# First mixture of experts: the down product fed in row slices one step behind the up product, summed by VectorE, with TensorE's program written out

## The chip, the cores and the metric

One Trainium2 chip, one of its cores. The metric is the time of one execution on the device in microseconds (us); lower is better. Everything is float32. TensorE ("PE" in the rows; "PEld" is its loading of weights) multiplies, VectorE ("DVE") and ScalarE ("ACT") work elementwise, GpSimd is "POOL", and SyncE ("SP") here does little but issue transfers from the chip's memory (HBM).

## The reference, cut to what matters

The program is a two-layer block (attention, feed-forward, attention, mixture of 8 experts), followed by a second block with a mixture of 32 small experts. The change touches only the first mixture, with 256 tokens of width 1024, hidden width 2816, two experts per token:

```python
logits = (x2 @ w_router).astype(jnp.float32) + b_router.astype(jnp.float32)
top_vals, top_idx = lax.top_k(logits, TOP_K)
gates = jax.nn.softmax(top_vals, axis=-1)
...
def expert_block(args):
    xb, e = args
    h = xb @ w_in[e]
    return (jax.nn.silu(h[:, :D_FF]) * h[:, D_FF:]) @ w_out[e]
...
y = jnp.zeros_like(x2).at[slot_tok].add((ys * slot_gate[:, None]).astype(x2.dtype))
```

All weights of an expert are read whatever its number of tokens: 1024 x 5632 and 2816 x 1024 floats, 22 and 11 times 1024 KB.

## The kernel before

Expert `e` has room for `CAPS[e]` tokens (80, 84, 60, 76, 64, 72, 68, 72). For each expert TensorE runs, in this order:

- **gather** (L1114, in `gather`): a 0/1 matrix picks the tokens' columns into `XG`, two more transposes turn the gates (L1119).
- **up** (L1166, in `up_half`, called by `up_pairs`): 11 steps `f`. Each uses 2 MB of weights `ein`, as two transfers of 1 MB (`x` = 0, 1), and makes 256 hidden columns and their 256 partners. The 1 MB slots of `IN1` are four, two steps deep. ScalarE applies silu (L2725), VectorE multiplies by the partner (L1715, `hn`), and all 22 hidden tiles are kept in `HT`.
- **down** (L1188, in `down`, called by `down_fours`): 8 steps `d`. Each uses 1408 KB of `eout`, which holds 128 output columns of all 2816 rows, and sums over all 22 hidden tiles inside PSUM, so it can't begin before the last up step. Its result is copied out by ScalarE (even `d`, `even_dims`) or VectorE (odd `d`, L2094). The slots `OUT1` are four.
- **turn** (L1148) and **scatter** (L821): the result is transposed back to tokens and multiplied by the gates; VectorE adds it to `Y`. They belong to expert `e - 1` and run inside expert `e`.

Each matrix product is issued as two halves of 64 output rows, and the profile has two MATMUL records for one product (the halves of float32). An expert has 1408 MATMUL records of up and 704 of down, and the same number of weight loads.

TensorE's program holds two loops per expert. `up_pairs` writes out two steps `f` and repeats them five times; `down_fours` writes out four steps `d` and repeats them twice. Waits inside the loops compare semaphores with registers that count up:

```python
with pe.Fori(16 * (5 * e + 1), 16 * (5 * e + 6), 16) as landed:
    for f in (1, 2):
        pe.wait_ge(hnD.sem, hid)
        for x in range(2):
            pe.wait_ge(loop_in[in_slot(f, x)], landed)
            up_half(e, f, x).then_inc(inP.sem, 1)
```

SyncE issues the transfers in one fixed order, each after a wait for its slot: for every expert all 22 transfers of `ein`, then all 8 of `eout` (`load_in`, L3084; `load_out`, L3088). The slots lie in `ringbuf`, which in the stages ahead of the mixture is a ring of four 2 MB slots; `cleared` names the product after which each of those is free. For the first expert four `ein` and two `eout` transfers are issued ahead, and `in_free(0, 0, x)` waits for ring slot 0, which the last product ahead of the mixture (the attention's output product, `wo`) empties last.

Of the kernel before, what the change touches and what calls it, by code (L numbers as in the profile page):

```python
# [16 lines left out]
NE1 = 8  # L17
# [266 lines left out]
def build(nc, dr, out, dbg=None):  # L284
    ctx = ExitStack()
    with ctx:
# [43 lines left out]
        F = lambda a: a.rearrange("p a b -> p (a b)")  # L330

# [22 lines left out]
        PGT = [ar(2048 + 256 * (e % 2), 256)[0:n, :] for e, n in enumerate(CAPS)]  # L354
        XG = [ar(2560 + 1024 * (e % 2), 8, n) for e, n in enumerate(CAPS)]
        HT = [ar(4608, 22, n) for n in CAPS]
        YT = [ar(7424, 8, max(CAPS))[:, :, 0:n] for n in CAPS]
        YS = [ar(8448 + 1024 * (e % 2), 1024)[0:n, :] for e, n in enumerate(CAPS)]
# [98 lines left out]
        ytA, ytD = [sig(n, ["free"] + [(e, i) for e in E8 for i in range(4)]) for n in ("yt_even", "yt_odd")]  # L457
        htA = sig("ht", [(2, q) for q in Q8])
        dnP = sig("exp_out", [(1, e, d) for e in E8 for d in range(8)] + [(2, q, i) for q in Q8 for i in range(2)])
# [102 lines left out]
        ring = Chunks(plan, slots1, s_ring, where, ends[2], (NE1, NE1, 2 * NE1, 2 * NE1))  # L562
        assert nu == ends[2] and ends[2] % RING != 3


        IN1 = [ringbuf[:, 2048 * k:2048 * k + 2048] for k in range(4)]
        OUT1 = [ringbuf[:, 8192 + DFF * k:8192 + DFF * k + DFF] for k in range(4)]
        first_in, loop_in = s_ring[0:2], s_ring2[0:4]
        loop_out = [s_ring[2], s_ring[3], s_ring2[4], s_ring2[5]]
        cleared = [plan[max(i for i in range(nu) if where[i] == k)][3] for k in range(RING)]  # L570
        at_loop = [max(v for s_, v in ring.value[0:nu] if s_ is s_ring[k]) for k in range(RING)]
        at_first, at_out = at_loop[0:2], at_loop[2]
        assert at_loop[2] == at_loop[3]

        def in_slot(f, x):
            return 2 * (f % 2) + x

        def in_free(e, f, x):

            if e == 0 and f < 2:  # L580
                return cleared[f % 2]
            return inP.at((1, e, f - 2, x) if f >= 2 else (1, e - 1, 10 if f == 0 else 9, x))

        def out_free(e, d):

            if e == 0 and d < 4:
                return cleared[3 if d else 2]
            return dnP.at((1, e, d - 4) if d >= 4 else (1, e - 1, 4 + d))

        loop_free = [inP.at((1, NE1 - 1, 10, 1)), inP.at((1, NE1 - 1, 9, 1)), dnP.at((1, NE1 - 1, 5)), dnP.at((1, NE1 - 1, 6))]  # L590
# [7 lines left out]
        base = [16 * 5 * NE1] * 4 + [max(n_ for s_, n_ in ring.value if s_ is s_ring[k]) for k in last] + [16 * 2 * NE1] * 2  # L598
# [31 lines left out]
        def plan_o1(e):  # L630
            return ([(dr["ein"][e, i].rearrange("x p n -> p x n"), SLOT) for i in range(11)],
                    [(dr["eout"][e, d], DFF) for d in range(8)])
# [173 lines left out]
        def tensor_program(pe):  # L806
# [325 lines left out]

            slot_ranks(1, NE1, cnt1)
            busy(1, 6)
            busy(1, 6, 256)
            gather(1, 0, [seD.at((1, 0))] * 2, PS, PG, XG)

            def turn(e):

                for h in range(2):  # L1140
                    pe.wait_ge(*ytA.at((e, 2 * h + 1)))
                    pe.wait_ge(*ytD.at((e, 2 * h + 1)))
                    if e + 1 < NE1:
                        pe.wait_ge(*(xgD.at((1, e + 1, 1)) if h else pgA.at((1, e + 1))))
                    else:
                        pe.wait_ge(*ctD.at(h))
                    for k in range(4):
                        ins = pe.transpose(PB[6 + h][0:CAPS[e], k * 128:(k + 1) * 128], YT[e][:, 4 * h + k, :], ident)  # L1148
                    ins.then_inc(*tuP.up((1, e, h)))

# [2157 lines left out]
```

## Time and profile before

| | |
|---|---|
| median of 3 runs | 1914.29 us (1910.86 to 1917.29) |
| the profiled execution | 1919.28 us, span 1917.4 us |
| busy share of the span | TensorE 91%, its weight loads 71%, VectorE 27%, ScalarE 13%, GpSimd 8% |
| first mixture | from 535.9 us to 1242.9 us of the span, 707 us |
| read there | 176 transfers of 1024 KB and 64 of 1408 KB, 276.8 MB |
| TensorE's granted clock | 0.99 in the mixture (full is 2.4 GHz) |

Times of rows are from the start of the span. "issue" as what ended an idle time means that the engine waited for nothing that the profile shows. The profile lists DMA queue by queue: q1 carries what SyncE issues, and the queue of the kind "instruction" carries the engines' own programs.

### The profile page before, as it was taken

To read this page: it belongs to the slowest core of one execution; us is meant where nothing else is said; L and a number is where in the kernel's file an instruction comes from. 1 tells how busy PE (TensorE), PEld (TensorE's weight loads), DVE (VectorE), ACT (ScalarE), POOL (GpSimd) and SP (SyncE) were. 2 spreads that over 40 slices of the span, in tenths; PEclk is the share of its full clock that TensorE was granted. 3 is DMA by queue.
4 is the path that set the end of the run, shared out by engine and by line. 5 is a ranking of instruction groups with operands and counts; after the bars stand their busy time and mean duration, and the time that the engine had idled before them with its cause. 6 is when DMAs were issued, how large, how long until landed. Compare 5 with 4: busy or idle time off the path is not lost.

```text
span 1917.4 us, 53202 instructions
## 1 busy us (share of the span) xinstructions
PE 1736.9 (91%) x24496; PEld 1359.0 (71%) x24496; DVE 520.8 (27%) x1257; ACT 249.8 (13%) x657; POOL 159.9 (8%) x307
## 2 busy tenths in 40 slices
PE   8999999999889998899889898899989989989775
PEld 7758885467489997788788888687657778643331
DVE  1641000233321111110101010246764343232223
ACT  2321000032101000000000000022133112010001
POOL 0000000000007400000000000065430000000000
PEclk9999999999999999999999999989989999999988
DMA  7225444241198999999999999932211028579996
GB/s 315 99 88 198 157 151 151 94 168 71 54 404 361 368 386 405 382 411 382 411 382 406 416 401 407 395 123 67 77 47 44 35 78 372 201 320 429 429 429 280
DMA packets 62950, 498.23 MB, mean 260 GB/s; under 512 B 7097, under 2 KB 15825, under 8 KB 17105
## 3 DMA queue, kind: packets, MB, share of 16 engines
q1 hardware_dynamic: 52672, 490.12, 63.6%
q10 hardware_dynamic: 10128, 5.97, 1.1%
q8 instruction: 111, 1.82, 0.4%
q14 instruction: 39, 0.31, 0.0%
HBM read 495.00 MB, written 1.05 MB: 259 GB/s over the span
## 4 chain that ended last, share of the span: by engine, by line
PE 70%; DMA 21%; DVE 4%; issue 3%; ACT 1%; ACTq 1%; SPq 0%; DVEq 0%
DMA ringbuf<-in_ein 13%; PE pb L812 11%; PE pb L1166 9%; PE pb L1188 8%; PE pb L821 7%; PE pb L817 5%; PE pb L885 3%; PE pb L1070 3%; DMA cst<-in_e2in 2%; PE pb L1387 2%; PE pb L1364 2%; PE pb L1653 2%; DMA ringbuf<-in_e2in 2%; PE pb L1114 2%; DMA ringbuf<-in_eout 2%
## 5 line engine op out<-in xcount | busy, mean ns | idle before, releaser
L1166 PE MATMUL pb<-arena,ringbuf 128*64 128x72 f32 (+6 forms) x11264 | 392.9, 229 | 50.7 <-DMA ringbuf<-in_ein 36.5
L1166 PEld LDWEIGHTS pb<-arena,ringbuf 128*64 128x64 f32 x11264 | 374.6, 138 | 68.9 <-issue 38.7
L1715 DVE TENSOR_TENSOR arena<-arena,pb 128x256 f32<-128x256 f32 (+9 forms) x130 | 46.5, 358 | 639.2 <-ACT arena L2725 394.4
L1188 PE MATMUL pb<-arena,ringbuf 128*64 128x72 f32 (+6 forms) x5632 | 187.5, 228 | 19.9 <-issue 17.1
L812 PE MATMUL pb<-XT,ringbuf 128*128 128x256 f32 (+2 forms) x1104 | 202.7, 346 | 0.8 <-ACT XT L2525 0.8
L1188 PEld LDWEIGHTS pb<-arena,ringbuf 128*64 128x64 f32 x5632 | 183.7, 138 | 24.0 <-issue 23.9
L812 PEld LDWEIGHTS pb<-XT,ringbuf 128*128 128x128 f32 (+1 forms) x1104 | 181.1, 193 | 22.1 <-issue 2.1
L2525 ACT ACTIVATE arena<-pb 128x256 f32<-128x256 f32 (+16 forms) x188 | 72.5, 404 | 528.7 <-PE pb L1188 176.0
L821 PE MATMUL pb<-arena 64*64 64x64 f32 (+9 forms) x664 | 106.1, 322 | 6.7 <-DVE Y L1715 4.2
L821 PEld LDWEIGHTS pb<-arena 64*64 64x64 f32 (+8 forms) x664 | 51.7, 152 | 57.7 <-issue 29.6
L817 PE MATMUL pb<-ringbuf,arena 128*128 128x512 f32 x192 | 85.0, 601 | 2.9 <-DVE arena L1715 1.8
L2725 ACT ACTIVATE arena<-pb 128x144 f32<-128x144 f32 (+6 forms) x88 | 25.6, 291 | 434.0 <-PE pb L1166 434.0
L885 PE MATMUL pb<-XT,ringbuf 128*128 128x256 f32 x336 | 77.7, 384 | 0.0
L885 PEld LDWEIGHTS pb<-XT,ringbuf 128*128 128x128 f32 x336 | 62.4, 191 | 11.8 <-issue 4.2
L817 PEld LDWEIGHTS pb<-ringbuf,arena 128*128 128x128 f32 x192 | 36.6, 193 | 47.7 <-issue 45.5
L2094 DVE COPY arena<-pb 128x72 f32<-128x72 f32 (+6 forms) x32 | 7.5, 233 | 199.4 <-PE pb L1188 199.4
L1364 PE MATMUL pb<-XT,ringbuf 128*128 128x256 f32 x224 | 56.7, 402 | 3.4 <-ACT arena L2525 3.4
L1715 DVE TENSOR_TENSOR Y<-Y,pb 128x512 f32<-128x512 f32 (+1 forms) x80 | 50.2, 633 | 30.5 <-PE pb L821 19.2
L1387 PE MATMUL pb<-XT,ringbuf 128*128 128x256 f32 x192 | 54.8, 403 | 1.6 <-ACT arena L2525 1.5
L1070 PE MATMUL pb<-ringbuf,arena 128*128 128x512 f32 x128 | 55.1, 592 | 0.0
L1114 PEld LDWEIGHTS pb<-arena,X 128*64 128x64 f32 (+1 forms) x768 | 46.6, 155 | 11.8 <-issue 7.4
L1364 PEld LDWEIGHTS pb<-XT,ringbuf 128*128 128x128 f32 x224 | 42.5, 198 | 14.2 <-ACT arena L2525 5.3
(408 smaller groups left out, 1800.0 us busy)
## 6 DMA issues: line engine op xcount, KB each, us to landing
ringbuf<-in_ein SPq DMA_DIRECT2D x176, 1024.0 KB, 7.5
ringbuf<-in_eout SPq DMA_DIRECT2D x64, 1408.0 KB, 9.6
arena<-in_e2in SPq DMA_DIRECT2D x13, 2048.0 KB, 26.4
ringbuf<-in_e2in SPq DMA_DIRECT2D x12, 2048.0 KB, 35.0
ringbuf<-in_fin SPq DMA_DIRECT2D x11, 2048.0 KB, 7.8
ringbuf<-in_e2out SPq DMA_DIRECT2D x8, 2048.0 KB, 30.8
ringbuf<-in_wo SPq DMA_DIRECT2D x6, 2048.0 KB, 7.8
arena<-in_e2out SPq DMA_DIRECT2D x6, 2048.0 KB, 33.4
```

The lines of the kernel that those rows point to most:

```text
L812: ins = pe.matmul(outp, w[:, j, col:col + m], rT[:, j, :], start=j == 0, stop=j == kt - 1)
L817: ins = pe.matmul(outp, aT[:, j, tt * 128:(tt + 1) * 128], w[:, j, col:col + n], start=j == 0, stop=j == kt - 1)
L821: return pe.matmul(o, l, r, start=True, stop=True)
L885: ins = pe.matmul(PB[b][:, i * 256:i * 256 + 256], held["p"][:, j, (col0 + i) * 128:(col0 + i + 1) * 128], xT[:, j, :], start=j == 0, stop ...
L1070: ins = pe.matmul(PB[2 * h + tt][:, :], hT[:, f, tt * 128:(tt + 1) * 128], w3[:, j, h * 512:(h + 1) * 512], start=f == 0, stop=False)
L1114: ins = pe.matmul(PB[b][h_, k * n:(k + 1) * n], x3[:, tt, dt_ * 128 + h_.start:dt_ * 128 + h_.stop], PS_[e][:, tt, :], start=tt == 0, stop ...
L1166: ins = pe.matmul(PB[4 + f % 2][h_, t * n:(t + 1) * n], w3[:, k, (t % 2) * 128 + h_.start:(t % 2) * 128 + h_.stop], XG[e][:, k, :], start= ...
L1188: ins = pe.matmul(PB[d % 2][h_, 0:CAPS[e]], w3[:, f, h_], HT[e][:, f, :], start=f == 0, stop=f == 21)
L1364: ins = pe.matmul(z_bank(k)[:, 0:256], w3[:, j, o:o + 128], xT[:, j, :], start=j == 0, stop=j == 7)
L1387: ins = pe.matmul(PB[5][:, 0:256], w3[:, j, br * 128:(br + 1) * 128], xT[:, j, :], start=j == 0, stop=j == 7)
L1715: return v.tensor_tensor(o, a, b, op)
L2525: return a.activation(dst, src, ACT.Copy, scale=1.0 if scale is None else scale)
```

## The change

The down product is cut the other way. `eout` is laid out by rows: step `s = 11 * e + f` needs the 256 rows that belong to the 256 hidden columns of up step `f`, 1 MB, and gives a partial sum for all 1024 output columns. It is computed one step behind the up product, in two PSUM banks (`PB[0]`, `PB[1]`), and VectorE adds each partial sum to `YT` in SBUF (the first one of an expert is copied). So `HT` shrinks to three hidden tiles `HID`, the eight copies of an expert (four on ScalarE, four on VectorE) go, and 22 operations of VectorE come. `ringbuf` has nine slots of 1 MB, three steps deep, six for `ein` and three for `eout`, and SyncE issues two `ein` and one `eout` per step, in one order through all 88 steps. The first slots wait for ring slots 1 and 2, or for nothing. TensorE's program has no loop: all 88 steps stand there one by one. Gather, turn and scatter move by some steps, and scatter uses three banks. The last copy and additions of the mixture fall to VectorE, before the turn of the last expert.

```diff
+        UP = (PB[4], PB[5], PB[3])
-        HT = [ar(4608, 22, n) for n in CAPS]
+        HID = [[ar(2816 + 16 * MC + 2 * MC * k, 2, n) for k in range(3)] for n in CAPS]
...
+        IN1 = [[ringbuf[:, 2048 * k:2048 * k + 2048] for k in pair] for pair in ((2, 3), (4, 5), (0, 1))]
+        OUT1 = [ringbuf[:, 2048 * k:2048 * k + 2048] for k in (8, 6, 7)]
...
+        def in_free(s, x):
+            if s < 3:
+                return cleared[(1, 2, 0)[s]]
+            return inP.at((1, *step_of(s - 3), x))
+        def out_free(s):
+            if s < 3:
+                return cleared[3] if s else None
+            return dnP.at((1, *step_of(s - 3)))
...
-            def up_pairs(e):
-                with pe.register(f"hid{e}") as hid:
-                    pe.reg_mov(hid, 11 * e + 1)
-                    with pe.Fori(16 * (5 * e + 1), 16 * (5 * e + 6), 16) as landed:
...
+            def up(e, f):
+                for x in range(2):
+                    pe.wait_ge(*in_there(11 * e + f, x))
+                    up_half(e, f, x).then_inc(*inP.up((1, e, f, x)))
+            def down_rows(e, f):
+                s, n = 11 * e + f, CAPS[e]
+                w3 = OUT1[s % 3].rearrange("p (k n) -> p k n", k=2)
+                for d in range(8):
+                    for k in range(2):
+                        for h_ in HALF:
+                            o = d * 128 + h_.start
+                            ins = pe.matmul(PB[d // 4][h_, (d % 4) * n:(d % 4 + 1) * n], w3[:, k, o:o + 64], HID[e][s % 3][:, k, :], start=k == 0, stop=k == 1)
+                return ins
+            def down(e, f):
+                pe.wait_ge(*hnD.at((1, e, f)))
+                pe.wait_ge(*out_there(11 * e + f))
+                pe.wait_ge(*read_before(e, f))
+                down_rows(e, f).then_inc(*dnP.up((1, e, f)))
+            def threes(e, f0, turns):
+                for f in range(f0, f0 + 3 * turns):
+                    up(e, f)
+                    down(e, f - 1)
...
+            def summed(s):
+                e, f = step_of(s)
+                v.wait_ge(*dnP.at((1, e, f)))
+                if f == 0 and e >= 2:
+                    for h in range(2):
+                        v.wait_ge(*tuP.at((1, e - 2, h)))
+                for h in range(2):
+                    part, got = F(YT[e][:, 4 * h:4 * h + 4, :]), PB[h][:, 0:4 * CAPS[e]]
+                    if f:
+                        v.wait_ge(*ytD.at((e, f - 1)))
+                    ins = tt_(part, part, got, ALU.add) if f else v.tensor_copy(part, got)
...
+                for f in range(11):
+                    s = 11 * e + f
+                    if s >= 3:
+                        load_in(who, s)
+                    if s >= 4:
+                        load_out(who if f else before_, s - 1)
```

TensorE (PE), third expert (60 tokens), before: up with its loop, scatter of the second expert (L821), gather for the fourth, down with its loop. A row in a loop stands once. A row's xN counts products.

```order
L1166 MATMUL pb<-arena,ringbuf 64x60 x64
L1148 MATMUL pb<-cst,arena 84x128 x8
L1174 UNCONDITIONAL_BRANCH
L1166 MATMUL pb<-arena,ringbuf 64x60 x64
L1180 REGISTER_ALU
L1166 MATMUL pb<-arena,ringbuf 64x60 x64
L1180 ISA
L1174 COMPARE_AND_BRANCH
L821 MATMUL pb<-arena 128x512 x4
L1114 MATMUL pb<-arena,X 64x76 x32
L1119 MATMUL pb<-cst,arena 76x128 x2
```

The same place now: up is L1205, down L1223, gather L1155, scatter L834, turn L1177.

```order
L834 MATMUL pb<-arena 128x512 x4
L1205 MATMUL pb<-arena,ringbuf 64x60 x64
L1223 MATMUL pb<-arena,ringbuf 64x84 x32
L1155 MATMUL pb<-arena,X 64x76 x32
L1205 MATMUL pb<-arena,ringbuf 64x60 x64
L1223 MATMUL pb<-arena,ringbuf 64x60 x32
L1162 MATMUL pb<-cst,arena 76x128 x2
L1177 MATMUL pb<-cst,arena 84x128 x8
L1205 MATMUL pb<-arena,ringbuf 64x60 x64
L1223 MATMUL pb<-arena,ringbuf 64x60 x32
L1205 MATMUL pb<-arena,ringbuf 64x60 x64
L1223 MATMUL pb<-arena,ringbuf 64x60 x32
```

The last pair of rows goes on, one for every step, where before two steps of up stood once and were repeated; each product now stands in the program by itself, and down's 32 products follow those of the next step's up.

SyncE (SP), from the last transfers ahead of the mixture into its first ones, before and then now (`in_wo` belongs to the product ahead):

```order
L3066 DMA ringbuf<-in_wo 128x4096 x2
L3084 DMA ringbuf<-in_ein 128x2048 x4
L3088 DMA ringbuf<-in_eout 128x2816 x2
L3091 DMA arena<-in_gb 128x2048
L3084 DMA ringbuf<-in_ein 128x2048 x18
L3088 DMA ringbuf<-in_eout 128x2816 x6
```

```order
L3117 DMA ringbuf<-in_wo 128x4096 x2
L3137 DMA ringbuf<-in_ein 128x2048 x2
L3144 DMA ringbuf<-in_eout 128x2048
L3137 DMA ringbuf<-in_ein 128x2048 x2
L3144 DMA ringbuf<-in_eout 128x2048 x2
L3137 DMA ringbuf<-in_ein 128x2048 x2
L3147 DMA arena<-in_gb 128x2048
L3137 DMA ringbuf<-in_ein 128x2048 x4
L3144 DMA ringbuf<-in_eout 128x2048
```

Nine transfers of 1 MB now stand ahead of the gains (`in_gb`), and the two kinds alternate from there on.

VectorE (DVE) within the first expert's last steps and the second's first, now (before, one L1715 of 128x160 per step stood there alone):

```order
L1761 TENSOR_TENSOR arena<-arena,pb 128x160
L1761 TENSOR_TENSOR arena<-arena,pb 128x320 x2
L1761 TENSOR_TENSOR arena<-arena,pb 128x168
L1761 TENSOR_TENSOR arena<-arena,pb 128x320 x2
L2003 COPY arena<-pb 128x240 x2
L1761 TENSOR_TENSOR arena<-arena,pb 128x168
L2145 COPY arena<-pb 128x336 x2
L2152 COPY arena<-pb 80x512
```

The two wide additions behind each narrow multiplication are the partial sums.

## Rows read from the trace of the kernel before

**Rows 1.** Busy time of each engine in the mixture, with counts of records.
```profile
core 0: us, PE busy (x) PEld busy (x) DVE busy (x) ACT busy (x) POOL busy (x), PEclk, DMA share, GB/s
535.80:1242.90 707.10, 635.71 (x17502) 591.38 (x17502) 88.21 (x265) 47.58 (x146) 59.42 (x150) 0.99 0.98 394
```

**Rows 2.** Waits from 530 to 1240 us: who for whom, us, times, longest.
```profile
PE pb L1166 <- DMA ringbuf<-in_ein: 36.5, 88, 2.0
...
PE pb L1188 <- issue: 17.1, 13, 2.1
PE pb L1166 <- issue: 12.5, 9, 2.3
...
PE pb L1188 <- DMA ringbuf<-in_eout: 2.6, 4, 0.8
```

**Rows 3.** DMA view, 530 to 1240 us: packets and MB; then transfers, KB, us to landing.
```profile
q8 instruction: 52, 0.85, 0.5%
...
ringbuf<-in_ein SPq DMA_DIRECT2D x172, 1024.0 KB, 7.5
ringbuf<-in_eout SPq DMA_DIRECT2D x62, 1408.0 KB, 9.1
```

**Rows 4.** TensorE's timeline, first expert: start, us, what, count [idle before <-what ended it].
```profile
535.86 2.30 PE L1166 MATMUL pb<-arena,ringbuf 128*64 128x80 f32 x60 [0.28 <-DVE arena L1957]
539.00 4.64 PE L1166 MATMUL pb<-arena,ringbuf 128*64 128x80 f32 x126 [0.85 <-issue]
544.41 4.64 PE L1166 MATMUL pb<-arena,ringbuf 128*64 128x80 f32 x127 [0.76 <-issue]
549.95 7.13 PE L1166 MATMUL pb<-arena,ringbuf 128*64 128x80 f32 x199 [0.90 <-issue]
...
588.00 4.85 PE L1166 MATMUL pb<-arena,ringbuf 128*64 128x80 f32 x128 [0.21 <-DMA ringbuf<-in_ein]
592.68 2.49 PE L1114 MATMUL pb<-arena,X 128*64 128x84 f32 x64
595.11 0.42 PE L1119 MATMUL pb<-cst,arena 128*84 128x128 f32 x2
595.45 8.58 PE L1188 MATMUL pb<-arena,ringbuf 128*64 128x80 f32 x241
606.03 4.17 PE L1188 MATMUL pb<-arena,ringbuf 128*64 128x80 f32 x115 [1.99 <-issue]
```

**Rows 5.** The chain that ended last: start, us, what; later experts and the end.
```profile
661.51 4.94 PE pb L1166 x128
...
676.44 4.93 PE pb L1166 x128
...
780.68 3.94 PE pb L1188 x127
784.62 2.10 issue
...
1237.00 1.01 PE pb L1148 x8
...
1238.97 3.87 PE pb L821 x8
```

**Rows 6.** DMA view, 200 to 300 us (feed-forward, no loops): packets and MB by queue.
```profile
q1 hardware_dynamic: 1032, 14.81, 40.4%
q8 instruction: 4, 0.07, 0.3%
```

**Rows 7.** SyncE's queue, 400 to 560 us: start, us from first to last, transfers.
```profile
427.83 19.81 SPq L3066 DMA_DIRECT2D ringbuf<-in_wo  x2
519.53 2.12 SPq L3084 DMA_DIRECT2D ringbuf<-in_ein  x4
```

**Rows 8.** VectorE's timeline near 480 and 534 us: one addition and one copy from PSUM.
```profile
480.26 0.55 DVE L1715 TENSOR_TENSOR scores<-pb,cst 128x384 f32<-128x384 f32 x1
...
534.16 0.49 DVE L1957 COPY arena<-pb 128x320 f32<-128x320 f32 x1 [1.51 <-PE pb L1114]
```

More of the change, by code:

```diff
@@ L571, in build @@
[L571 to L588, printed above, removed]
@@ L590, in build @@
-        loop_free = [inP.at((1, NE1 - 1, 10, 1)), inP.at((1, NE1 - 1, 9, 1)), dnP.at((1, NE1 - 1, 5)), dnP.at((1, NE1 - 1, 6))]
+        NS1 = 11 * NE1
+        fills = [len(range(k, NS1, 3)) for k in range(3)]
+        ring = Chunks(plan, slots1, s_ring, where, ends[2], (fills[2], fills[0] + 1, fills[1] + 1, fills[2] + 1))
+        assert nu == ends[2]
+        IN1 = [[ringbuf[:, 2048 * k:2048 * k + 2048] for k in pair] for pair in ((2, 3), (4, 5), (0, 1))]
+        OUT1 = [ringbuf[:, 2048 * k:2048 * k + 2048] for k in (8, 6, 7)]
@@ L597, in build @@
         last = [where[n1 - RING + i] for i in range(RING)]
-        base = [16 * 5 * NE1] * 4 + [max(n_ for s_, n_ in ring.value if s_ is s_ring[k]) for k in last] + [16 * 2 * NE1] * 2
+        filled = [level + 16 * n for n in fills + fills[0:2]] + [0]
+        base = filled[0:4] + [max(n_ for s_, n_ in ring.value if s_ is s_ring[k]) for k in last] + filled[4:]
         ring2 = Halves(plan2, late, s_ring2[0:4] + [s_ring[k] for k in last] + s_ring2[4:], base)
@@ L1135, in tensor_program, with turn @@
             busy(1, 6, 256)
-            gather(1, 0, [seD.at((1, 0))] * 2, PS, PG, XG)
-            def turn(e):
+            gather1(0, [seD.at((1, 0))] * 2)
+            gates_turn(0, seD.at((1, 0)))
+            def turn(e, free):
+                pe.wait_ge(*ytD.at((e, 10)))
                 for h in range(2):
[L1141 to L1146, printed above, removed]
+                    pe.wait_ge(*free[h])
                     for k in range(4):
@@ L1221, in tensor_program @@
+                up(e, 1)
+                down(e, 0)
+                if e == 0:
+                    gather1(1, [xgD.at((1, 0, 0)), xgD.at((1, 0, 1))])
+                if e + 1 < NE1:
+                    gates_turn(e + 1, acD.at((1, e - 2, 1, 1)) if e >= 2 else pgA.at((1, e)))
+                if e:
+                    turn(e - 1, [xgD.at((1, e + 1, h)) if e + 1 < NE1 else btA.at(h) for h in range(2)])
                 if e + 1 < NE1:
-                    gather(1, e + 1, [ysA.at((1, e - 1)), ysD.at((1, e - 1))] if e else [pgA.at((1, 0)), xgD.at((1, 0, 1))], PS, PG, XG)
-                else:
-                    s5_turn(dup, [btA.at(0), btA.at(1)], "dup", ctP)
@@ L1230, in turned_again @@
+            down(NE1 - 1, 10)
+            turn(NE1 - 1, [ctD.at(0), ctD.at(1)])
+            scatter1(NE1 - 1, acD.at((1, NE1 - 2, 1, 1)))
             def turned_again():
```

242 lines of the change are left out of this document (129 added, 113 removed).

## The prediction

> **What bounds the kernel now.** I read four views. The busy times per stretch come first [rows 1]: in the mixture's 707.1 us TensorE has a product running for 635.7 us, its clock is at 0.99, VectorE works for 88 us and ScalarE for 48 us. So TensorE idles 71.4 us, and the DMA engines hardly at all (share 0.98), and they move 394 GB/s. Two resources are nearly full side by side. The waits say what ends TensorE's idle times [rows 2]: data in 92 cases, 36.5 + 2.6 = 39.1 us, and "issue" in 22 cases, 17.1 + 12.5 = 29.6 us, up to 2.3 us each. That second kind is what this change acts on, and it needs two more views. The DMA view counts 52 packets of the kind "instruction" on q8 in the mixture, 0.85 MB, 16.4 KB each [rows 3]. TensorE's timeline shows where the issue times fall [rows 4]: at 539.00, 544.41 and 549.95 us, with 126 and 127 MATMUL records between them. They are in the last written-out step ahead of the loop and in the loop's first pass. At 588.00 us, in a later pass, 128 records take 4.85 us and the pause ahead ends with data. 17,502 records [rows 1] at 127 each would be 138 stretches, of which only 52 are new code, which fits the 52 packets. I read this as: one 16 KB block of program holds 64 products (128 records); it is fetched by the same DMA engines that carry the weights; and when TensorE meets a block for the first time, it waits if the block hasn't come. Later passes of a loop find it there.
>
> The Trainium skill's page "Runtime: NRT & Kernel Launch", section "Instruction fetch mechanics", describes such blocks: 16 KiB, 256 instructions, fetched by the sequencer through DMA while the block before runs. The block size agrees with these rows. The same section calls the fetch mostly hidden, says that a taken branch breaks it, and says that kernels therefore prefer full unrolling. That speaks for this change, and against my forecast; it is rival A below.
>
> **What a new block costs.** Between 539.00 and 549.95 us two blocks take 5.41 and 5.54 us for 4.64 us of products, with pauses of 0.85, 0.76 and 0.90 us [rows 4]. With 60 tokens the products of a block take 3.94 us, and the pause behind is 2.10 us: 6.04 us in sum [rows 5]. So what is constant is more the time of a fetch, 5.4 to 6.0 us from one block's start to the next one's, than the pause. It is the loaded DMA queue that makes it so long: from 200 to 300 us, where the queue is busy 40% of the time, four blocks are fetched [rows 6] and no pause of that kind is in the waits (there a block lasts 25 us, so this only bounds the fetch from above). After a loop the next block is there: from 592.68 us on, the gather's 66 records and down's first 241 [rows 4] run without a pause, and 1.99 us follow. So of the 52 blocks 16, one at each loop's exit, came free, and the other 36 paid 29.6 us: **0.82 us each**, in line with the 0.84 us mean of the first expert's three. Two bounds: 29.6 / 52 = 0.57 us, and 1.32 us, the mean of the five pauses printed here (0.85, 0.76, 0.90, 1.99, 2.10 [rows 4, 5]).
>
> **The change part by part.**
> - Loops gone: products and records stay the same in number (up 1408, down 704 per expert), but all 138 blocks are new. In a straight program no block comes free by a loop's exit. 138 x 0.82 = 113.2 us of pauses in place of 29.6 us.
> - Order and slots: the data waits of 39.1 us go. Bytes stay at 276.8 MB. Three steps in the middle of up, from 661.51 to 676.44 us, take 14.93 us for 6.29 MB [rows 5], 421 GB/s, so all bytes need 657 us, 4.76 us per block. TensorE with 635.7 us of products and 113.2 us of pauses is slower than that, and six to nine filled slots stand ready for it. Cost of a data wait: nothing, covered by TensorE's own 749 us; if that cover goes (rival A), the 657 us bind.
> - First loads: of the nine transfers five no longer wait for ring slot 0, whose wait ended at 519.53 us [rows 7], and SyncE has nothing else from 447.6 us on (427.83 + 19.81). They bring the data stream forward by 5 x 2.49 = 12 us, the two `eout` of slots 6 and 7 a little more. TensorE starts at 535.86 us [rows 4] either way, for the router's results. Worth nothing while TensorE binds.
> - VectorE: two operations of 240 to 336 columns from PSUM per step, between 0.49 us (320 columns, copy) and 0.55 us (384, addition) [rows 8]: 88 x 1.0 = 88 us more beside its 88 us in 707. What hides it: the partial sum `s` is needed when down `s + 1` starts, and up `s + 2`, 64 products of 3.9 to 4.9 us, lies between. Without that cover it would be 1.0 us per step, 88 us. ScalarE loses 32 copies, off the path.
> - Down's own products: the same weights of 64 columns and the same token counts, so the same 704 records and their time; zero, and I see no reason for a gain or a loss. Gather, turn and scatter are moved, not removed. Scatter's four products (3.87 us [rows 5]) get a third bank, worth up to 0.5 us each, 4 us in all; I take 0 and keep it in the range. At the very end two additions instead of one copy stand between the last product and the turn (1.01 us [rows 5]): +1.5 us.
> - SyncE: per step three transfers, 264 instead of 240, each behind a wait for its slot; a transfer waits behind one for an earlier slot only, in the order in which TensorE empties them. Nothing.
>
> **Sum.** 635.7 + 113.2 + 1.5 = 750.4 us, against 707.1: +43.3 us. The profiled execution's 1919.28 us would become 1962.6. It lies 5.0 us above the median of 1914.29, to which I apply the difference: 1957.6, say **1958 us**.
>
> **Rivals.**
> A. The program is fetched far enough ahead when nothing branches, so the pauses vanish. For: the pauses of before all lie near a loop's entry or exit, and each could be put down to it. Against: the first expert's pause at 539.00 us comes before the first branch back of its loop. Time: the first two experts are bound by TensorE, 16.5 blocks of 4.85 and 4.94 us [rows 4, 5] and 7.8 us each for gather, turn and scatter (2.49 + 0.42 [rows 4], 1.01 and 3.87 [rows 5]), 174 us; then six experts at 82 us of data, 492, less 22 us for nine full slots; plus 9 us of tail (turn, scatter, the last down step and its sums): 653 us, 54 less. **1860 us.** It decides if a fetch takes under the 3.9 us of a block's products.
> B. The fetch gets shorter because the queue is emptier. Now up to three transfers stand behind each other (7.5 us to landing for 2.49 us of transfer [rows 3]); with TensorE slower than the data, slots come free singly. Price down to 0.57: 138 x 0.57 = 79, sum 716, +9. **1923 us.** For: the constant seems to be the queue's. Against: as TensorE catches up with the data, the queue fills again.
> C. Every block pays the large pause, as those met under a full queue did (2 us at 606 and 784 us), or VectorE's 88 us come onto the path. At 1.2 us per block, between the price taken and the bound, the pauses are 166 us and the sum is 803, +96. **2010 us.** Against: the pauses empty the queue.
>
> By the Trainium skill's rule ("Runtime: NRT & Kernel Launch", "Instruction fetch mechanics") rival A would be the likeliest. By the rows I give it less, since they show a fetch of 5.4 us in straight code.
>
> **How the numbers follow.** Forecast (+25 to +75 us) 0.55; A 0.15; B (-15 to +25) 0.17; C 0.13. A measurement of this kernel can tell about 0.3%, 5.7 us, from no change. Faster: A and a fifth of B, 0.18. Within 0.3%: 0.07. Slower: 0.75. The range leaves out A and the end of C, about 0.2: 1895 to 2025 us. It takes in the lower price (+9) with the scatter's 4 us, and a price of 1.3 us per block (+109), next to the upper bound.
>
> **What would show it.** In the profile after: instruction packets on q8 in the mixture near 138 instead of 52, 2.3 MB; the program's own total 86 higher. In TensorE's waits "issue" near 110 us in over 80 cases, and data under 10 us. In the timeline of a middle expert, pauses every 127 to 128 records, longer where there are fewer tokens, so that a block takes 5.0 to 5.8 us whatever the tokens. DMA near 370 GB/s in the mixture, where it was 394, and no stretch at 421. Experts of 60 tokens as long as those of 80. I am wrong if pauses are rare (A), if they are as many but short (B), or if waits for VectorE appear ahead of down. If DMA moves over 410 GB/s in the mixture, the data bound it after all.

## The result, and the profile of the kernel after

The change makes the kernel slower by 5%: 2010.28 us median of four runs (1996.9 to 2016.81) against 1915.54 us for the kernel before in the same session (1910.86 to 1917.29), a ratio of 1.049, with a 95% interval from 1.045 to 1.054. The direction was forecast and the time lies in the range, but the loss is 94.7 us where 43 was forecast: more than twice. It is the size of rival C, and a part of it, the lower clock, was in no rival.

The profiled execution took 2016.81 us, 97.5 more than the one of before. The busy times per stretch, with the stretch's bounds first, put all of that into the mixture; it is the row that answers to [rows 1]:

```profile
core 0: us, PE busy (x) PEld busy (x) DVE busy (x) ACT busy (x) POOL busy (x), PEclk, DMA share, GB/s
534.90:1341.80 806.90, 652.08 (x17502) 611.05 (x17502) 152.68 (x407) 41.56 (x116) 59.17 (x150) 0.96 0.93 345
```

The mixture starts at 534.90 us (before: 535.80) and takes 806.9 us, 99.8 more than the 707.1 of [rows 1]; behind it the two kernels differ by under 2 us. The number of records is the same, 17,502. Their time grew from 635.71 to 652.08 us, the clock fell from 0.99 to 0.96, and the DMA engines moved 345 GB/s, where it was 394. VectorE works 64 us more.

TensorE's waits from 530 to 1345 us (who for whom: us in total, times, longest) answer to [rows 2]:

```profile
PE pb L1205 <- issue: 93.3, 66, 3.2
PE pb L1223 <- issue: 53.3, 37, 2.8
PE pb L1155 <- issue: 4.4, 3, 1.6
PE pb L1223 <- DVE arena L1761: 1.0, 1, 1.0
PE pb L834 <- DVE arena L2152: 1.0, 1, 1.0
PE pb L1177 <- DVE arena L1761: 0.9, 1, 0.9
PE pb L834 <- issue: 0.8, 1, 0.8
```

The four rows with "issue" make 93.3 + 53.3 + 4.4 + 0.8 = 151.8 us in 107 cases, where there were 29.6 us in 22. No wait for data is left, where there were 39.1 us. VectorE holds TensorE up for about 1 us at three places, all at the very end (two more waits for it, of 0.3 and 0.2 us, lie at the start and were there before).

The DMA view from 530 to 1340 us answers to [rows 3]:

```profile
q8 instruction: 138, 2.26, 1.0%
...
ringbuf<-in_ein SPq DMA_DIRECT2D x170, 1024.0 KB, 7.4
ringbuf<-in_eout SPq DMA_DIRECT2D x85, 1024.0 KB, 7.4
```

There are 138 instruction packets, the number worked out from the records (the window's bounds decide on one or two of them). The program's own total rose by 85, from 111 to 196.

TensorE's timeline in the first expert, 80 tokens wide (start, us, what, count, and in brackets the idle time ahead of it), answers to [rows 4]:

```profile
563.75 0.50 PE L1205 MATMUL pb<-arena,ringbuf 128*64 128x80 f32 x8 [1.72 <-issue]
564.02 2.44 PE L1223 MATMUL pb<-arena,ringbuf 128*64 128x80 f32 x64
566.24 2.16 PE L1205 MATMUL pb<-arena,ringbuf 128*64 128x80 f32 x56
568.95 2.71 PE L1205 MATMUL pb<-arena,ringbuf 128*64 128x80 f32 x72 [0.55 <-issue]
571.49 2.10 PE L1223 MATMUL pb<-arena,ringbuf 128*64 128x80 f32 x55
574.64 0.51 PE L1223 MATMUL pb<-arena,ringbuf 128*64 128x80 f32 x9 [1.05 <-issue]
574.97 4.31 PE L1205 MATMUL pb<-arena,ringbuf 128*64 128x80 f32 x119
580.01 0.51 PE L1205 MATMUL pb<-arena,ringbuf 128*64 128x80 f32 x9 [0.73 <-issue]
```

Count the records from one bracket to the next: 8 + 64 + 56 = 128, 72 + 55 = 127, 9 + 119 = 128. A pause comes every 64 products, in the middle of a step or of a product's group, wherever a block of the program happens to end. The pauses come 5.20, 5.69 and 5.37 us after each other.

The trace also keeps the time of every DMA packet, and these tie the pauses to the program directly. Each of the 107 pauses ends 1.2 to 1.6 us after an instruction packet of q8 has ended (median 1.41 us). The packet itself takes only about 0.95 us. So more than half of the 5.2 to 5.7 us from one block to the next passes before the packet's own transfer begins.

The stretches from one turn to the next, each one expert's worth of work (84, 60, 76 and 64 tokens in this order; columns as in the first row above), show what stays constant:

```profile
644.30:745.20 100.90, 85.15 (x2196) 80.11 (x2194) 20.15 (x47) 4.30 (x13) 22.66 (x53) 1.00 0.93 344
745.20:848.90 103.70, 79.29 (x2196) 74.86 (x2195) 17.36 (x48) 4.00 (x13) 0.00 (x0) 0.93 0.92 336
848.90:945.20 96.30, 80.16 (x2197) 75.66 (x2196) 18.77 (x47) 4.20 (x13) 0.00 (x0) 0.98 0.97 361
945.20:1049.20 104.00, 78.57 (x2197) 74.06 (x2195) 17.78 (x48) 4.04 (x13) 0.00 (x0) 0.93 0.93 339
```

2196 records are 17.2 blocks, so a block takes 5.9, 6.0, 5.6 and 6.1 us. The expert of 60 tokens takes longer than the one of 84. TensorE's arithmetic doesn't set the time here; the arrival of its program does. In the experts of fewer tokens the clock also stands lower.

### The profile page after: what moved, and what is told of

It is laid out like the page before. It is cut to its first block, busy times and chain, and to the rows that moved or that the text cites. A ratio compares the mean times of both kernels' runs of the same rounds, so it can differ in the third digit from the quotient of the medians.

```text
span 2015.0 us, 53113 instructions
## 1 busy us (share of the span) xinstructions
PE 1753.6 (87%) x24496; PEld 1378.5 (68%) x24496; DVE 585.2 (29%) x1402; ACT 242.1 (12%) x625; POOL 159.5 (8%) x307
## 4 chain that ended last, share of the span: by engine, by line
PE 81%; issue 8%; DMA 5%; DVE 4%; ACT 1%; ACTq 0%; SPq 0%; DVEq 0%
PE pb L1205 20%; PE pb L825 11%; PE pb L1223 10%; PE pb L834 7%; PE pb L830 4%; PE pb L898 3%; PE pb L1083 3%; PE pb L1410 2%; PE pb L1433 2%; DMA cst<-in_e2in 2%; PE pb L1699 2%; DMA ringbuf<-in_e2in 2%; PE pb L1726 2%; PE pb L1421 1%; PE pb L1363 1%
## 5 line engine op out<-in xcount | busy, mean ns | idle before, releaser
L1205 PE MATMUL pb<-arena,ringbuf 128*64 128x72 f32 (+6 forms) x11264 | 411.9, 233 | 93.7 <-issue 93.3
L1205 PEld LDWEIGHTS pb<-arena,ringbuf 128*64 128x64 f32 x11264 | 392.3, 142 | 112.2 <-issue 111.6
L1761 DVE TENSOR_TENSOR arena<-arena,pb 128x256 f32<-128x256 f32 (+15 forms) x290 | 111.9, 409 | 850.3 <-ACT arena L2776 429.2
L1223 PE MATMUL pb<-arena,ringbuf 128*64 128x72 f32 (+6 forms) x5632 | 217.1, 234 | 54.3 <-issue 53.3
L1223 PEld LDWEIGHTS pb<-arena,ringbuf 128*64 128x64 f32 x5632 | 203.8, 143 | 59.1 <-issue 59.0
L834 PE MATMUL pb<-arena 64*64 64x64 f32 (+9 forms) x664 | 110.3, 330 | 7.5 <-DVE Y L1761 4.2
L2584 ACT ACTIVATE arena<-pb 128x256 f32<-128x256 f32 (+8 forms) x156 | 65.0, 439 | 343.9 <-PE pb L1132 64.1
L834 PEld LDWEIGHTS pb<-arena 64*64 64x64 f32 (+8 forms) x664 | 54.6, 154 | 57.8 <-issue 40.0
L1795 DVE SCALAR_TENSOR_TENSOR Y<-X,pb 128x512 f32<-128x512 f32 x16 | 11.0, 688 | 137.7 <-PE pb L830 69.6
```

What stands on the lines that cost most here:

```text
L834: return pe.matmul(o, l, r, start=True, stop=True)
L1205: ins = pe.matmul(UP[f % 3][h_, t * n:(t + 1) * n], w3[:, k, (t % 2) * 128 + h_.start:(t % 2) * 128 + h_.stop], XG[e][:, k, :], start=k == ...
L1223: ins = pe.matmul(PB[d // 4][h_, (d % 4) * n:(d % 4 + 1) * n], w3[:, k, o:o + 64], HID[e][s % 3][:, k, :], start=k == 0, stop=k == 1)
L1761: return v.tensor_tensor(o, a, b, op)
L2584: return a.activation(dst, src, ACT.Copy, scale=1.0 if scale is None else scale)
```

## Experiments

Nine kernels were run. The first four ask whether the written-out program is the cause, and of what the pause is made; the rest ask what holds the fetch up, and whether a kernel with loops can gain from that. In all of them "issue" pauses are those of TensorE in the mixture, and the price per block is their sum over 138 blocks (70 where the loop of three steps is in). Every such pause ends 1.2 to 1.7 us after an instruction packet, except for some in the two kernels with at most two transfers on their way, which are told apart there.

### The kernel before, written out

Nothing of the change but its last part: both of TensorE's loops become straight code. Order, slots, copies and transfers are those of before.

```diff
-                    with pe.Fori(16 * (5 * e + 1), 16 * (5 * e + 6), 16) as landed:
-                        for f in (1, 2):
-                            pe.wait_ge(hnD.sem, hid)
-                            for x in range(2):
-                                pe.wait_ge(loop_in[in_slot(f, x)], landed)
+                for f in range(1, 11):
+                    pe.wait_ge(hnD.sem, 11 * e + f)
+                    for x in range(2):
+                        pe.wait_ge(loop_in[in_slot(f, x)], 16 * (5 * e + 1 + (f - 1) // 2))
...
-                    with pe.Fori(16 * (2 * e + 1), 16 * (2 * e + 3), 16) as landed:
-                        for d in range(4):
+                for d in range(8):
+                    landed = 16 * (2 * e + 1 + d // 4)
```

> The kernel before, with one edit: both of TensorE's loops per expert are written out (10 up steps, 8 down steps, waits on constants); order, transfers, slots, layout and sums are those of before. Theory T (a 16 KB block of program that is met for the first time costs TensorE a pause, because its fetch takes 5 to 6 us behind the weight transfers): 138 instruction packets in the mixture instead of 52, pauses of kind issue of 120 to 170 us instead of 30, time 1990 to 2020 us. Rival R (the pauses come from the new order: three kinds of waits per step, small transfers, VectorE's sums): time within 10 us of before, pauses near 30 us.

Measured: 2014.37 us (2010.65 to 2022.01), a ratio of 1.0525 with an interval from 1.049 to 1.056. The mixture's row, and two of TensorE's waits:

```profile
535.00:1339.70 804.70, 656.19 (x17504) 613.15 (x17502) 88.71 (x266) 47.65 (x146) 59.23 (x150) 0.96 0.90 349
```

```profile
PE pb L1166 <- issue: 93.9, 69, 2.9
PE pb L1184 <- issue: 44.0, 27, 3.0
```

The whole loss comes from writing the loops out: this kernel has the old order, the old copies and the old slots, and its mixture of 804.7 us is within 3 us of the changed kernel's 806.9. The same pauses are there (138.9 us, 1.01 us per block, with 1.0 us at the gather), and the same fall of the clock. Theory T holds with its time and its pauses, and rival R falls. New order, nine slots and 64 us of VectorE are worth nothing measurable under this bound. The data waits are nearly gone here too, 7.8 us instead of 39.1, in the old order and with the old slots: TensorE has become slow enough for the data.

### The kernel after, with a loop of three steps

The rest of the change with the loop back: of each expert's eleven steps nine run as three turns of a loop (in the last expert two turns), with registers for the levels that the waits need.

```diff
+                    with pe.Fori(level + 16 * (low + 1), level + 16 * (low + 1 + turns), 16) as landed:
+                        for f in range(f0, f0 + 3):
+                            ...
+                                up_half(e, f, x).then_inc(inP.sem, 1)
+                            pe.wait_ge(hnD.sem, hid)
+                            pe.wait_ge(out_sem[(s - 1) % 3], at(s - 1))
+                            pe.wait_ge(ytD.sem, got)
+                            down_rows(e, f - 1).then_inc(dnP.sem, 1)
```

> The changed kernel, with one edit: in every expert the nine (in the last expert six) steps f from 2 (5) on are a TensorE loop of three steps that is passed three times (twice), waits against registers; nothing else. T: 526 products stand written out per expert instead of 1102, so 66 to 70 packets instead of 138; one block per loop's exit is free, 58 to 62 blocks pay 1.1 us, 64 to 68 us of pauses instead of 152; the mixture takes 650 + 66 = 716 us, the kernel 1915 to 1930 us. R: as the changed kernel, 2000 to 2015 us.

Measured: 1908.04 us (1905.2 to 1913.15, seven runs), a ratio of 0.9972 with an interval from 0.9956 to 0.9987. It is the fastest kernel with all of its computation, by 5 us over the one before. The time lies 7 us under what I had expected (1915 to 1930), and the pauses, 74.0 us, above it (64 to 68). The larger miss was in the products: I took the 650 us of the written-out kernel, and they took 618.9.

```profile
534.90:1231.00 696.10, 618.92 (x17503) 588.51 (x17502) 155.26 (x409) 40.38 (x114) 59.47 (x150) 0.98 0.98 396
```

```profile
PE pb L1205 <- issue: 40.1, 30, 2.5
PE pb L1223 <- issue: 32.0, 21, 2.8
PE pb L1155 <- issue: 1.9, 2, 1.1
```

The timeline of TensorE in one expert shows the boundary between new and known program:

```profile
823.81 0.88 PE L1223 MATMUL pb<-arena,ringbuf 128*64 128x76 f32 x21 [1.81 <-issue]
824.52 3.72 PE L1205 MATMUL pb<-arena,ringbuf 128*64 128x76 f32 x107
829.27 0.94 PE L1205 MATMUL pb<-arena,ringbuf 128*64 128x76 f32 x21 [1.03 <-issue]
829.99 2.33 PE L1223 MATMUL pb<-arena,ringbuf 128*64 128x76 f32 x64
832.09 4.44 PE L1205 MATMUL pb<-arena,ringbuf 128*64 128x76 f32 x128
836.30 2.33 PE L1223 MATMUL pb<-arena,ringbuf 128*64 128x76 f32 x64
```

Up to 829.27 us the loop's first pass pays at every block; from there on 576 records per turn run with no bracket at all. The body of 4.5 blocks stays at hand from turn to turn. The busy times of 35 us in those turns show that the weights alone hold nothing up: TensorE never idles while the DMA engines are full.

```profile
835.00:870.00 35.00, 35.00 (x1070) 35.00 (x1065) 6.90 (x18) 1.79 (x6) 0.00 (x0) 1.00 1.00 417
```

Over the whole mixture two things are nearly full side by side. The DMA engines have a share of 0.98 and move 396 GB/s, as before. TensorE's products and its pauses fill all but 3 of the 696.1 us, and it never waits for data. So the new order did remove the 39 us of data waits, but 44 us more of pauses took their place (70 packets of program in the mixture instead of 52), and the gain is in the products, 618.9 us instead of 635.7. In sum this kernel gains 5 us.

### An eighth and a half of the bytes

Twice the kernel after, with transfers that bring only part of each row from step 3 on (the later steps then work partly on stale weights). Program, order and number of transfers stay.

```diff
+                    w_ = 2048 if s < 3 else 256
-                    sp.dma_start(IN1[s % 3][x], dr["ein"][who, f, x].rearrange("o p n -> (o p) n"))
+                    sp.dma_start(IN1[s % 3][x][:, 0:w_], dr["ein"][who, f, x].rearrange("o p n -> (o p) n")[:, 0:w_])
```

> The changed kernel, but from the fourth step on each of the mixture's weight transfers brings only the first 256 of 2048 columns of its slot (an eighth of the bytes), so the products use stale weights; instructions, waits and order are the same, 138 blocks. T, with the queue as the cause: fetches take under 3 us, below the 3.8 to 4.9 us of a block's products, pauses of kind issue fall from 152 to under 15 us, the kernel takes 1855 to 1870 us. Rival F (a fetch takes 5 to 6 us by itself): pauses stay at 130 to 160 us, 1995 to 2015 us.

> As the run with an eighth of the bytes, with half of them (1024 of 2048 columns per transfer from the fourth step on). T: the queue is busy for about half of the time and a fetch waits for at most one or two transfers of 1.25 us, so it takes 2.5 to 4 us: pauses of 10 to 40 us, 1860 to 1890 us. F: pauses of 130 to 160 us.

Measured: 1811.72 us with an eighth (256 columns), 1862.32 us with a half (1024 columns), one run each. The mixture's row and TensorE's waits, first of the eighth:

```profile
534.90:1137.20 602.30, 597.08 (x17524) 574.74 (x17519) 153.76 (x410) 40.37 (x114) 59.45 (x150) 1.00 0.25 71
```

```profile
PE pb L1223 <- issue: 1.4, 2, 1.1
```

then of the half:

```profile
534.90:1188.60 653.70, 610.37 (x17502) 581.03 (x17502) 153.27 (x407) 39.94 (x114) 59.23 (x150) 1.00 0.69 219
```

```profile
PE pb L1205 <- issue: 28.8, 33, 2.3
PE pb L1223 <- issue: 10.3, 13, 1.7
```

With an eighth, T's pauses came true (under 15 us) and its time did not: 1811.72 us where 1855 to 1870 was expected, again because the products took less time (597.1 us) than I had put in. With a half, pauses (39.6 us) and time lie in T's ranges.

The written-out program costs nothing by its length alone: all 138 blocks are fetched in the kernel with an eighth too, and 1.7 us of pauses remain. The price per block is 1.10 us with all bytes, 0.29 us with half, 0.01 us with an eighth. What is late is the fetch, and what makes it late is the traffic of the weights. A fetch of a fixed length (rival F) is refuted.

### Transfers in two halves

The kernel after with each 1 MB transfer issued as two of 512 KB: once by columns (4 KB of each of 128 rows), once by partitions (8 KB of 64 rows).

```diff
-                    sp.dma_start(IN1[s % 3][x], dr["ein"][who, f, x].rearrange("o p n -> (o p) n")).then_inc(in_sem[s % 3][x], 16)
+                    for c in (slice(0, 1024), slice(1024, 2048)):
+                        sp.dma_start(IN1[s % 3][x][:, c], dr["ein"][who, f, x].rearrange("o p n -> (o p) n")[:, c]).then_inc(in_sem[s % 3][x], 16)
```

> The kernel after, with each weight transfer of the first mixture (1 MB, 128 rows of 8 KB) issued as two of 512 KB that bring half of every row: packets of 4 KB in place of 8 KB, twice as many transfers, the same bytes and the same computation. Three ways in which the fetch of TensorE's next 16 KB block may be held up. B (by bytes: it waits behind all weight bytes that its DMA engine holds): 1.10 us per block as in the kernel after, 140 to 165 us of pauses, 2000 to 2025 us. P (by packets: it waits behind a set number of weight packets, now half as long): 0.4 to 0.8 us per block, 55 to 110 us of pauses, 1930 to 1985 us. D (by transfers: the one under way has to end): the same fall as P. My theory is B, with P next.

> The kernel after, with each weight transfer issued as two of 512 KB that bring 64 of the 128 rows: packets stay at 8 KB, transfers are halved; the same bytes and computation. B: 1.10 us per block, 140 to 165 us of pauses, 2000 to 2025 us. P: the same as B, since the packets are as long as before. D: 0.4 to 0.8 us per block, 1930 to 1985 us. Beside the kernel with halved rows this one tells P from D.

Measured by columns: 2033.56 us (2033.01 to 2034.11), ratio 1.0625 with an interval from 1.055 to 1.070. By partitions: 2424.45 us, ratio 1.267 (1.258 to 1.275). The waits by columns, then by partitions with the mixture's row:

```profile
PE pb L1205 <- issue: 99.1, 61, 3.4
PE pb L1223 <- issue: 54.9, 36, 3.1
```

```profile
PE pb L1205 <- issue: 260.9, 78, 5.5
PE pb L1223 <- issue: 154.8, 45, 5.2
```

```profile
534.90:1750.00 1215.10, 783.85 (x17502) 733.24 (x17502) 153.06 (x408) 41.66 (x116) 59.21 (x150) 0.85 1.00 229
```

By columns the pauses are 99.1 + 54.9 and 3.7 at two other lines, 157.7 us or 1.14 us per block, inside what theory B gave (140 to 165). Halving both packets and transfers made no fetch shorter, so P and D fall as I had stated them. The time of 2033.56 us is 9 us above B's range. The run by partitions missed every expectation: a transfer into 64 partitions moves so slowly that the DMA engines are full at 229 GB/s, and so it doesn't keep all else equal and can't tell P from D. What it does show fits the same picture from the other end: with the weights slower, the pauses are 428.3 us with those of two other lines (9.3 and 3.3), 3.1 us per block. It also tells between two causes that the runs with fewer bytes leave open. Fewer bytes per second come from the memory here than in the kernel after (229 GB/s instead of 345), and the pauses are nearly three times as long; so it is the occupied DMA engines that delay the fetch, and not the rate at which the memory is read.

### At most two transfers on their way

The kernel after, with SyncE holding each transfer back until the one two before it has landed.

```diff
                     sp.wait_ge(*in_free(s, x))
+                    if s >= 3:
+                        sp.wait_ge(*(in_there(s - 1, 1) if x == 0 else out_there(s - 2)))
```

> The kernel after, with one more wait on SyncE ahead of every weight transfer of the first mixture from step 3 on: the transfer two before it must have landed, so at most two (2 MB) are on their way, where landing in 7.4 us at 343 GB/s means about 2.5 MB on average. B: pauses fall in proportion to the bytes on their way, to some 0.7 to 0.9 us per block (95 to 125 us), and the time to 1970 to 1995 us if TensorE does not begin to wait for data. P and D: no change of the price per block (140 to 165 us). What each would leave open: if data waits appear, their sum stands apart from the pauses in the view of waits.

Measured: 2014.94 us (2006.22 to 2023.67, two runs), ratio 1.053 with an interval from 1.040 to 1.066. TensorE's waits:

```profile
PE pb L1205 <- issue: 61.5, 52, 2.7
PE pb L1223 <- issue: 39.8, 41, 2.6
PE pb L1205 <- DMA ringbuf<-in_ein: 34.3, 41, 2.7
PE pb L1223 <- DVE arena L1761: 11.8, 10, 1.6
```

The rows with "issue" hold 61.5 + 39.8 + 0.9 = 102.2 us in 95 cases, but not all of it is program. By the times of packets and landings in the trace, 79 of the pauses (92.2 us) end 1.2 to 1.6 us after an instruction packet. The other 16 (10.0 us) end 0.09 us after a weight transfer has landed, and are waits for `eout`. So the price is 92.2 / 138 = 0.67 us per block, with the transfers landing in 5.8 us instead of 7.4. It fell as B said, and slightly below its 0.7 us; P and D, which gave no change, fall again. The time did not fall: 34.3 + 10.0 us of waits for data and 11.8 us for VectorE took the place of the 59.6 us saved, and B's time (1970 to 1995 us) did not come, since its condition, that TensorE does not begin to wait for data, did not hold. The two runs lie 17 us apart, so a small difference to the kernel after can't be told.

### The loop of three steps, with an eighth of the bytes

The kernel with the loop and the eighth's transfers (again, the later steps work partly on stale weights).

> The kernel with TensorE's loop of three steps, with weight transfers that bring an eighth of their bytes from step 3 on (the products of the mixture then work on stale weights). It asks what a loop costs by itself once no fetch is late, beside the written-out kernel at the same bytes (1811.7 us, 1.7 us of pauses). T (the pause is only the late fetch, and a turn of the loop is free): 1806 to 1816 us, pauses under 4 us, about 70 blocks. Rival L (each jump back costs its own 0.5 us or more; there are 15): 1819 us or more, with pauses at the first products of a turn.

Measured: 1809.77 us (1807.69 to 1811.86). The mixture:

```profile
534.90:1135.50 600.60, 597.17 (x17570) 576.01 (x17569) 155.61 (x414) 40.37 (x114) 59.23 (x150) 1.00 0.22 68
```

No "issue" pause is in TensorE's waits. The rows of both kernels begin at 534.9 us, ahead of their first products. From the first product to the last it is 597.3 us with the loop and 601.0 without: a turn of the loop costs nothing, T holds, and L falls.

### The loop of three steps, with two transfers on their way

The kernel with the loop, and the same two waits in SyncE's program as above.

> The kernel with TensorE's loop of three steps, with SyncE's extra wait so that at most two transfers are on their way. Theory M (this kernel is bound by its weight transfers, 396 GB/s at a busy share of 0.98, and its 74 us of pauses lie beside them): the pauses fall to 45 to 65 us, and the time does not: 1906 to 1930 us, the lost ground showing as waits of TensorE for in_ein or as idle time of the DMA engines. Rival S (the pauses are on the path): 1885 to 1900 us, faster than with the full queue by the pauses saved.

Measured: 1968.01 us (1961.86 to 1977.46, four runs), ratio 1.0265 with an interval from 1.023 to 1.030.

```profile
PE pb L1205 <- DMA ringbuf<-in_ein: 53.1, 81, 2.5
PE pb L1223 <- issue: 34.4, 47, 3.0
PE pb L1205 <- issue: 22.5, 20, 2.3
PE pb L1223 <- DVE arena L1785: 14.7, 13, 1.6
```

Here too a row with "issue" need not be a fetch. This one, in a turn of the loop where the program is at hand, ends 0.09 us after a weight transfer has landed:

```profile
807.16 2.08 PE L1223 MATMUL pb<-arena,ringbuf 128*64 128x60 f32 x64 [0.50 <-issue]
```

The "issue" rows hold 57.2 us in 68 cases. 36 of them (39.9 us) follow an instruction packet, and the other 32 (17.4 us) end 0.09 us after a landing, so they are waits for `eout`. The pauses for program fell from 74.0 to some 40 us, more than M's 45 to 65, and the time rose by 60 us: waits for data (53.1 + 17.4 us) and for VectorE (14.7) came in, and the mixture's weights moved at 356 GB/s instead of 396. Both expected times missed, M's 1906 to 1930 and S's 1885 to 1900. I had M's direction, but a queue of two transfers costs the data stream far more than I gave it. The run doesn't decide between M and S: in the kernel with the full queue the pauses do stand on TensorE's path, and this run took some of them away only by adding other waits. What it shows is that a queue of two transfers doesn't buy the pauses off.

### What the runs show together

| kernel | price per block, us | products, us | clock | mixture, us |
|---|---|---|---|---|
| eighth of the bytes | 0.01 | 597.1 | 1.00 | 602.3 |
| half of the bytes | 0.29 | 610.4 | 1.00 | 653.7 |
| two transfers on their way | 0.67 | 645.1 | 0.99 | 796.3 |
| after | 1.10 | 652.1 | 0.96 | 806.9 |
| two by columns | 1.14 | 662.0 | 0.95 | 823.0 |
| two by partitions | 3.10 | 783.9 | 0.85 | 1215.1 |

These six have the new order, written out. The rows behind the table start at 534.9 us, up to 4 us ahead of a kernel's first product. The kernel before, written out, has 1.01 us per block, 656.2 us of products and 804.7 us.

The products' own time goes from 597 to 784 us, for two reasons that the traces show. One is the clock: it stands at its lower level (1.2 instead of 2.4 GHz) for 68.6 us of the kernel after's mixture, hardly at all with half of the bytes and 374.5 us in the last line. The other is the restart: by the profile's times a single record lasts 0.23 us, and the next ones normally begin some 0.03 us after each other, so that after every wait of TensorE, whatever it was for, some 0.2 us of this overlap are lost and counted as products. With 111 waits that makes 24 us in the kernel after and about 34 us more for the clock, which is the 55 us by which its products exceed those of the eighth.

## Why the prediction was right in direction and short by half

By its own steps:

- **What bounds the kernel, and blocks of 64 products.** Right to within a packet: 138 blocks, +85 in the whole program (86 forecast), pauses every 127 or 128 records.
- **What a new block costs: 0.82 us.** This is the step that failed. It measured 151.8 / 138 = 1.10 us, which is 151.8 us of pauses instead of 113.2, 38.6 us of the shortfall. The divisor was wrong: the step took 16 of the 52 blocks of before as free, one at each loop's exit, and let the other 36 share the 29.6 us. But [rows 2] count 22 such pauses, so 30 blocks came free, and a pause cost 29.6 / 22 = 1.35 us. It costs nearly the same now, 151.8 / 107 = 1.42 us. What rose is the share of blocks that pay: 107 of 138, where it was 22 of the forecast's 36. The paragraph also held a better way itself: it said that the time of a fetch is what is constant, 5.4 to 6.0 us from block to block, and then summed with a mean of pauses. That mean was taken over the paying blocks of before, and its cross-check was three blocks of the expert with 80 tokens, where the products cover 4.64 us of the fetch. Six of the eight experts have fewer than 80. With 5.7 us per block, the middle of what the text gave, the mixture would have been 138 x 5.7 = 787 us, +80. Measured is 806.9 / 138 = 5.85 us. The bound of 1.32 us did hold it.
- **Records stay the same, and so does their time.** Right in number; in time 16.4 us short (652.1 instead of 635.7). I carried the 0.99 clock of [rows 1] into a mixture with five times the "issue" pauses. The clock stood at its lower level for 68.6 us, where it was 10.2 before, and that is worth some 28 us. So at one clock the records would have taken about 12 us less than before, for which no run shows the reason. At the very end the clock can be seen on a single row: scatter's eight records take 7.16 us, at a granted clock of 0.50, where they took 3.87 in [rows 5]. First the row of the timeline, then the one of the busy times for the same stretch.

```profile
1334.62 7.16 PE L834 MATMUL pb<-arena 72*128 72x512 f32 x8 [0.98 <-DVE arena L2152]
```

```profile
1334.60:1341.80 7.20, 7.16 (x8) 2.49 (x8) 2.06 (x3) 1.49 (x2) 0.00 (x0) 0.50 0.91 385
```

- **Data waits vanish.** Right: 39.1 us became none, with nine slots filled ahead of a TensorE that the program holds back. The slower TensorE alone did most of it (7.8 us in the old order, written out), and with loops the new order did it too.
- **First loads, ScalarE, down's products, SyncE: nothing.** Right as far as the trace tells.
- **VectorE hidden, +1.5 us at the end.** Right: 64 us more work (88 forecast, so the price per operation was high), no wait in the steady part, and three waits of about 1 us at the end, of which the scatter's was there before. Of the scatter's possible 4 us nothing is to be seen (its products took 34.7 us, before 31.0); its last one lost 3.3 us to the clock.
- **Rival A.** Refuted, and the runs say why: its condition, a fetch under the 3.9 us of a block's products, does come true with an eighth of the bytes (1.7 us of pauses), but not under the full weights. (Its working has a slip that changes little: 16.5 blocks each of 4.85 and 4.94 us and twice 7.8 us make 177 us, not 174.) The Trainium skill's sentence that the fetch is mostly hidden ("Runtime: NRT & Kernel Launch", "Instruction fetch mechanics") holds in that kernel (1.7 us over 138 blocks) and in no kernel here whose DMA engines are busy for 0.9 of the time or more. The same section's preference for full unrolling is what the first experiment contradicts: 1914 us with loops, 2014 us without.
- **Rival B.** The queue did get emptier (0.93 instead of 0.98), and the landing, at 7.4 us, stayed what it was (7.5); the price did not fall.
- **Rival C.** Its number came true, 2010 us, with one of its two mechanisms: large pauses (1.10, where it said 1.2) and no VectorE on the path. That the time agrees to the microsecond is luck: its pauses (166 us) were 14 us too many, and the 16.4 us of longer product time, which it didn't have, made up for them.
- **What would show it.** Blocks of 5.0 to 5.8 us were forecast; 5.6 to 6.1 are there. "Issue" near 110 us in over 80 cases was forecast; it is 151.8 in 107. DMA near 370 GB/s was forecast; it is 345. Experts of 60 tokens as long as those of 80: yes.

The sum of the steps against the measurement: 750.4 + 38.6 (price) + 16.4 (time of the records) = 805.4, and 1.5 us stay unassigned. The sum closes because the time of the records is taken as one term; inside it the clock's 28 us and the 12 us gained elsewhere partly cancel.

## What to carry to other kernels

Where TensorE runs through new code beside a full weight stream, sum with the time from one program block to the next, and not with a mean of the pauses: the pause is that time less the products of the block, so it grows where the work per instruction shrinks. And count how many blocks paid, instead of assuming it: a price per block taken from a kernel with loops is diluted by blocks that came free. On this kernel, whose weight stream fills the DMA engines, a loop whose body stays at hand is worth 5% over the same code written out, and its turns are free. A change of order that takes waits away should be tried with the loops kept: here the new order with a loop gained 5 us, while the same order written out lost 95. And an idle time marked "issue" should be held against the times of the instruction packets before it is called a fetch.

## What the runs showed of the hardware

- The fetch of a TensorE program block shares the DMA engines with the kernel's own traffic and has no precedence that keeps it short: 0.01, 0.29 and 1.10 us of pause per block at DMA shares of 0.25, 0.69 and 0.93. It depends on the depth of the queue too (0.67 us with at most two transfers on their way), and not on the size of packets as such (1.14 us with half packets). By which rule a DMA engine takes the packets of the two queues stays open.
- The delay lies ahead of the packet's own transfer: a packet of 16 KB takes 0.95 us at the median in the kernel after, 1.0 us in the one before and 1.3 us with transfers by partitions. A pause for program ends 1.2 to 1.7 us after the end of its packet in every kernel here.
- The weights suffer as well. The kernel after moves 345 GB/s at a share of 0.93, which would be 371 at 1.00; the kernel with the loop moves 396 at 0.98, or 404. So each byte takes the engines 9% longer. In the kernel before, written out, it is 349 at 0.90, or 388, 4% longer. I did not find out why.
- Transfers into 64 of 128 partitions are slow: the same bytes, with the engines full, move at 229 GB/s instead of 371. The size of 512 KB isn't the reason, since halves by columns move at 338 GB/s at a share of 0.94.
- A loop body of 4.5 blocks stays at hand: its later turns fetch nothing and pause nowhere, also with the DMA engines at a share of 1.00.
- In the written-out kernels with full weights the granted clock falls to its lower level (1.2 instead of 2.4 GHz) for short stretches in the middle of the mixture (0.93 over an expert of 60 tokens), and stays at 1.00 with half of the bytes. The sum of TensorE's idle times doesn't order the kernels by it: the loop with two transfers on their way has 129 us of them at a clock of 1.00, and the loop with the full queue 77 us at 0.98. What makes the clock fall was not tested and stays open.
